# Eighteen or twenty-two cache copies beside the out-projection, and what they wait for

## What is computed

```python
q, k, v = split(rms_norm(x) * (1 + sc1) + sh1) @ w_in       # two groups of 8 heads
oa = stick_breaking(q_a, [paged cache, k_a], [paged cache, v_a])   # samples read 16 pages each of keys, values
ob = dilated_attention(q_b, [window cache, k_b], [window cache, v_b])
x  = x + g1 * (concat(rms_norm(oa), rms_norm(ob)) @ w_out)  # the out-projection
h  = rms_norm(x) * (1 + sc2) + sh2
expert = top-16 of 16384 for each token and each of 8 heads  # product keys
x  = x + g2 * sum(g * gelu(expert_u[expert] . h) * expert_v[expert])
y  = rms_norm(x) * norm_final
dil_k_sample, dil_v_sample = window caches, moved up by one row
```

## Time and profile before

| | |
|---|---|
| median of 3 runs | 1243.59 us (1243.56 to 1243.82) |
| profiled execution | 1251.91 us, span 1250.2 us |
| PE, DVE, ACT, POOL busy | 75%, 51%, 28%, 33% of the span |
| bytes moved by DMA | 481.3 MB, mean 385 GB/s |
| chain that ended last | DMA 23%, PE 9%, issue 5%, DVE 3% |

### The profile page before, as it was taken

The page is one execution under the profiler, slowest core; times in us unless marked ns, Lnnn a source line. Parts: engine busy times, 40 slices in busy tenths (PEclk is TensorE's granted clock), DMA queues, the critical chain, the costliest instruction groups (busy, mean ns, idle before and its releaser), DMA issues. The chain is left out here.

```text
span 1250.2 us, 13002 instructions
## 1 busy us (share of the span) xinstructions
PE 932.9 (75%) x3662; PEld 435.7 (35%) x3662; DVE 636.6 (51%) x1604; ACT 350.6 (28%) x959; POOL 408.1 (33%) x431
## 2 busy tenths in 40 slices
PE   2896986568755497698697887767867778777784
PEld 0442432344322145454253443322323223332331
DVE  3200106643221253846555656566777776777755
ACT  0000001562120101232323323323334443344333
POOL 2101323113221000243342424334545455554541
PEclk9798987868885788799998888988989999999986
DMA  9999999998999932799999999999999999999996
GB/s 369 426 374 381 356 365 358 393 340 350 391 429 375 414 123 84 290 380 428 428 427 427 425 428 430 427 428 427 428 378 426 428 427 427 428 428 428 428 427 275
DMA packets 72834, 481.30 MB, mean 385 GB/s; under 512 B 9953, under 2 KB 10306, under 8 KB 27346
## 3 DMA queue, kind: packets, MB, share of 16 engines
q0 software_dynamic: 54864, 378.58, 73.8%
q1 hardware_dynamic: 17922, 102.12, 20.6%
HBM read 477.41 MB, written 70.32 MB: 438 GB/s over the span
## 5 line engine op out<-in xcount | busy, mean ns | idle before, releaser
L974 PE MATMUL ps<-R,diag 128*128 128x512 f32 x1024 | 507.9, 648 | 158.9 <-ACT diag L1288 158.9
L1800 DVE CUSTOM_DVE_ANT_0 R<-R,H 128x1024 f32<-128x1024 f32 x264 | 320.3, 1223 | 221.4 <-DMA R<-in_uv,idst 211.1
L486 POOL DMA_INDIRECT R<-in_uv,idst x256 | 299.1, 1168 | 393.3 <-PE ps L974 349.3
L974 PEld LDWEIGHTS ps<-R,diag 128*128 128x128 f32 x1024 | 204.5, 207 | 448.7 <-ACT diag L1288 225.3
L1261 ACT ACTIVATE gel<-dots 128x2 f32<-128x2 f32 x132 | 26.8, 203 | 395.7 <-DVE dots L1800 395.7
L587 PE MATMUL ps<-R,HT 128*128 128x512 f32 x192 | 95.1, 635 | 3.8 <-DMA R<-in_wts 3.8
L1288 ACT ACTIVATE diag<-const,wgt 128x128 f32<-128x128 f32 x256 | 88.9, 394 | 9.2 <-PE ps L974 0.6
L750 PE MATMUL ps<-R,ast 128*32 128x512 f32 x256 | 42.6, 742 | 45.0 <-DMA R<-in_sb_v,vrow 44.5
L313 POOL DMA_INDIRECT R<-in_sb_v,vrow x32 | 30.6, 955 | 125.8 <-PE ps L750 102.1
L1264 ACT ACTIVATE wgt<-gel,gst 128x1 f32<-128x1 f32 x264 | 63.3, 287 | 4.3
L304 POOL DMA_DIRECT2D R<-in_sb_k x64 | 34.8, 544 | 89.2 <-issue 88.6
(11 more groups left out here) (284 smaller groups left out, 846.7 us busy)
## 6 DMA issues: line engine op xcount, KB each, us to landing
R<-in_wts POOLq DMA_DIRECT2D x48, 1024.0 KB, 12.8
out_dil_k_s<-in_dil_k SPq DMA_DIRECT2D x32, 1023.5 KB, 7.8
out_dil_v_s<-in_dil_v SPq DMA_DIRECT2D x32, 1023.5 KB, 7.9
R<-in_sb_k SPq DMA_DIRECT2D x64, 256.0 KB, 8.8
R<-in_sb_k POOLq DMA_DIRECT2D x64, 256.0 KB, 6.9
R<-in_win_v SPq DMA_DIRECT2D x8, 512.0 KB
R<-in_uv,idst POOLq DMA_INDIRECT x256, 12.3
m_all<-in_win_k SPq DMA_DIRECT2D x6, 512.0 KB
```

Of the source, the lines that this page charges most:

```text
L486: pool.indirect_dma_start(out=R[:, row_slot(k), :], out_offset=None, in_=A["uv"], in_offset=bass.IndirectOffsetOnAxis(ap=idst[:, par, k:k ...
L974: last = pe.matmul(ps[:, banks + q, :], diag[:, k % 4, :], R[:, row_slot(k), D + q * 512:D + (q + 1) * 512], start=False, stop=False, skip ...
L1800: dve.tensor_tensor_reduce(u, u, H[:, t, :], 1.0, 0.0, ALU.mult, ALU.add, dots[:, k:k + 1]).then_inc(s["dot_done"], 1)
```

## The change

Before the copies 20 and on, SP gets a wait for `v_used` at (8 - 1) x 4 + 1 = 29: PE has used the first value quarter of the last sample. And `PACED` is 42 in place of 38: 22 copies follow this wait untied, and 22 in place of 26 are tied to the expert rows, the first again at `e_used` 1, the last at 85 in place of 101.

```diff
-EARLY, GAP, PACED, PACE = 16, 20, 38, 4
+EARLY, GAP, PACED, PACE = 16, 20, 42, 4
...
                 window_rows(sp, DV, b, b % 2, A["win_v"], dv_ready)
                 window_end(sp, DV, b, b % 2, A["dil_v_s"], dv_ready)
+            sp.wait_ge(s["v_used"], (NB - 1) * VQ + 1)
             copies(GAP, PACED, 2)
             sp.wait_ge(s["h_ready"], 6)
```

## The result

The changed kernel takes 1204.22 us at the median of 4 executions (1201.46 to 1208.45), against 1243.7 for the kernel before (1243.56 to 1257.17). The ratio is 0.966, with a 95% interval of 0.959 to 0.973. The forecast was 1203.3 us. The median of the kernel before was 4.4 to 8.7 us higher when it was measured again beside the experiments (1248.1, 1252.4 and 1251.6 us), so the difference of 39.5 us between the two medians is uncertain by several us.

A forecast was written before the change was run, and what follows sets the result against it. DMA was taken to bound the expert rows, and waits for value quarters to delay the first gather; 31 (tail) + 9.8 (fewer tied copies) - 0.5 (sub-keys) = 40.3 us off 1243.59 gives 1203.3 us, range 1195 to 1214.

The forecast's parts named there:

- The account of bytes: From 367.66 to 449 us: 32.2 MB moved, 18.9 of it copies; no backlog beyond 4.9 MB at the start.
- Rival 1: Tail: value quarters stay slow from latency, not sharing; only the 9.8 us remain, less up to 2: 1235 us; 5%.
- Sample 6's first quarter: Tail: without copies it lands 2.4 us sooner, so PE's wait of 8.32 us falls to 5.9.
- Waits, in sum: Tail: PE's 35.2 us of waits for value quarters in the last two samples shrink by 27.7 us.
- The clock term: Tail: PE work at the higher clock after fewer waits saves 3 us, of 9.7 if all went to the high level.
- rival 5: Tail: all of the low clock goes and landings are fast; tail gain 37 us, sum 47, time 1197 us; 15%.
- 22 copies fit ahead of the first gather: Before the first gather near 478 us: copies from about 390 us end at 459 to 470, in idle DMA time.
- rival 3: Around the first gather: the 22 copies overrun it, costing 2.45 us per copy in the expert rows; 1213 us; 5%.
- The sub-keys: Before the scores: their load meets copies in flight, costing 0 to 2 us, taken as 0.5.
- Four tied copies fewer: Expert rows: 4.2 MB less at 427 GB/s in the DMA-bound phase saves 9.8 us, at least 7.
- Rival 2: Expert rows: the freed bytes bring nothing because rows after the copies' end go by the engines; 1213 us; 6%.
- Rival 4: Between 437 and 509 us: denser PE work is held at 1.2 GHz, up to 48 us more; 1251 us; 2%.

The follow-up runs named there:

- the first two experiments: Against the kernel before: the added wait with 18 copies behind it and 26 tied, 1214.62 us; then 22 untied copies without the wait, 1244.7 us.
- the wait alone: The kernel before plus only the added wait, with 18 copies behind it and 26 tied to expert rows: 1214.62 us, ratio 0.9715.
- The wait at 25: The changed kernel with the added wait four quarters earlier, at PE's first quarter of sample 6: 1231.58 us, ratio 0.9826.
- the experiment with those weights last: The changed kernel with the out-projection's 4 MB loaded after the last sample's quarters, query weights waiting until they landed: 1211.33 us, ratio 0.9691.

## Why the prediction was right

The time was forecast 0.9 us off, and so near a hit is luck in part. 40.3 us were forecast; the first measurement has 39.5 between the medians, the later one 45.8 (1251.6 and 1205.9 us), and the two profiles, without the 8.5 us ahead of the last window rows, 41.9. As a ratio the forecast is 0.968, within both intervals (0.959 to 0.973, 0.955 to 0.969). By its own steps:

- **The bound.** Right. DMA is at 422 and 427 GB/s in the two long stretches of the expert rows in both kernels, and the two terms, an earlier first gather and fewer bytes behind it, were separated by the first two experiments (30.4 and 10.1 us in their stretches). By the time, the second term is 8.8 to 10.4 us between the wait alone and the changed kernel (two medians), but only 4 without the wait.
- **The account of bytes** at 367.66 us, by which nothing but sharing slowed the quarters: right for what the copies met. The wait at 25 brings the slow quarters back (27 us); 22 copies without the wait do so too. Rival 1 falls. But the account began too late for sample 6: its quarters shared with the out-projection's weights before a copy was near.
- **Sample 6's first quarter** was put at 2.4 us sooner (wait 5.9 us). Wrong: the wait is 8.62, and 8.9 with no copy near, against 8.32 before. It stands behind the out-projection's weights, as the experiment with those weights last shows, so this term's gain was zero.
- **Waits, in sum.** 27.7 us forecast; 35.2 less 10.5 (10.3 for quarters, 0.2 for DVE) is 24.7 measured. 2.7 of the missing 3 are the step above.
- **The clock term**, taken as 3 of a possible 9.7 us: mis-sized, by 5 to 6 us. Without its waits the tail has 61.5 - 35.2 = 26.3 us of work before and 28.0 - 10.5 = 17.5 after: 8.8 us, at a granted clock of 0.62 before and 0.82 after:

```profile
365.30:426.86 61.56, 26.33 (x116) 9.26 (x114) 6.63 (x23) 3.92 (x11) 4.87 (x6) 0.62 1.02 405
...
356.80:384.87 28.07, 17.57 (x115) 6.89 (x115) 6.48 (x23) 3.71 (x11) 4.89 (x6) 0.82 0.99 400
```

  PE was at the lower level (1.2 GHz) only from 365 to about 372 us, behind the 8.6 us wait, and at the upper (2.4 GHz) from 373 us on. Of the 9.7 us by which rival 5 counted the clock, 8.8 came, though the low clock did not go altogether. The tail is 33.5 us shorter for 31, the two errors partly cancelling; by a second profile of the changed kernel it is 30.7, of which 22.5 are waits and 8.1 faster work.
- **22 copies fit ahead of the first gather.** Nearly right. They took 3.85 us each (380.65 to 461.59), not 3.1 to 3.6, and moved at 355 GB/s where 396 and 346 were the bounds. The last was issued at 461.59 and, at the 7.3 to 8.7 us that the copies then took, landed 2 to 3 us after the first gather was issued, so rival 3 showed only as a trace: two copies in flight at the first gather, a sign named for it, and the rows no longer for it. It is full: four more were given back.
- **The sub-keys**, 0 to 2 us, taken as 0.5: 0.52 in this profile, 1.1 in the second. The landing, 12.5 us, was over the bound of 11. The cover that was named (11.7 us) didn't quite hold, so that scores waiting for the sub-keys, named as a sign of being wrong, did show, at half a microsecond. The 18.9 against 13.3 MB from which the prediction read the copies' larger share prove nothing: the quarters were issued only as PE freed their slots, so 13.3 MB is what was asked for. The shares show in the landings, 12.5 us here and more with three copies in flight or a later start (waits of 16.0 and 4.3 us).
- **Four tied copies fewer**, 9.8 us: 9.7 in the stretch to the first finish. Another 1.3 us came back behind it, of the size by which that last stretch differs among kernels that are alike in it (342.3 to 344.5). Rival 2 falls.
- **Which time the sum starts from.** The change was taken over to the median, and this came out; the span of 1210 it also named was missed (1199.8). The profiled execution of before was 8.3 us over its median, and the table puts 8.5 us between the two profiles ahead of the last window rows, where the kernels don't differ. What makes that early stretch vary was not found, and so the forecast could not tell which length the measured executions would have.
- **Rival 4** (a lower clock in the out-projection): 0.90 over the copies' stretch, no sign of it.

## What to carry to other kernels

Bulk transfers that nobody waits for belong where DMA is idle and not where an engine starves for loads. Compare the bandwidth by slice with the waits for DMA: 18 copies cost about 31 us beside the value quarters, 22 cost 0.6 to 1.9 beside the out-projection, and in the DMA-bound phase each costs its bytes at full rate (2.3 to 2.45 us), no more. Count how much fits: past that point more of them, or more in flight, turns into somebody's wait. And where a wait for DMA goes, price the clock of the work behind it too; here that was 8.8 of the tail's 33.5 us.

## What the runs showed of the hardware

A transfer issued by POOL beside copies issued by SP got less than an even share. The 1 MB of sub-keys landed in 6.6 to 7.0 us with no copy beside it, in 11.9 to 16.1 us with two copies in flight all the while, and in 27.9 with three. The Trainium skill ("DMA: Bandwidth & Descriptors", the section SWDGE vs HWDGE vs iDMA) says that a DMA engine takes its internal queues in turn. Read as an even split of the bytes, this would make the transfer 5.3 us in place of 2.6, about 9.3 to landing (an estimate from the 6.6); the runs don't agree. Why three in flight more than double the landing stays open, and whether it is the queue or the kind of transfer (the copies go from DRAM to DRAM, the sub-keys don't) was not told apart.

Stretches filled mostly by DRAM-to-DRAM copies moved 325 to 376 GB/s at a DMA share of 0.90 to 1.02, with two in flight or three, while gathers mixed with such copies ran at 422.

TensorE's granted clock followed the waits: 0.62 in the tail with 35.2 us of them, 0.67 with 30.3, 0.82 with 10.3; a value quarter took 1.93 us behind a long wait and 1.06 in unbroken work.
